# Down projection of a ConvFFN by Strassen's scheme at one level, its weight blocks split by ScalarE, GpSimd and VectorE

## The reference, cut to what matters

```
u = rmsnorm(x, g_pre_ffn) @ w_up                       # 1024 -> 2 * 2816
uc = conv_b + sum over i of u_ext[:, i:i+T] * conv_w[i]   # width 3, per channel
gate, val = uc[..., :2816], uc[..., 2816:]
f = (gelu(gate) * val) @ w_down                        # 2816 -> 1024
x = x + rmsnorm(f, g_post_ffn)
```

## Time and profile before

| | us |
|---|---|
| median of 3 runs (lowest 1851.1, highest 1852.47) | 1851.71 |
| the profiled execution's own time | 1849.15 |
| its span, first to last instruction | 1847.4 |
| PE busy | 1824.8 |
| POOL busy | 1075.4 |
| DVE busy | 923.5 |
| ACT busy | 559.5 |

### The profile page before, as it was taken

The page is one execution under the profiler, slowest core; times in us unless marked ns, Lnnn a source line. Parts: engine busy times, 40 slices in busy tenths (PEclk is TensorE's granted clock), DMA queues, the critical chain, the costliest instruction groups (busy, mean ns, idle before and its releaser), DMA issues.

```text
span 1847.4 us, 33704 instructions
## 1 busy us (share of the span) xinstructions
PE 1824.8 (99%) x14214; PEld 1768.4 (96%) x14214; DVE 923.5 (50%) x1634; ACT 559.5 (30%) x1197; POOL 1075.4 (58%) x996
## 2 busy tenths in 40 slices
PE   9999999999999999999999999999999999999999
PEld 8999889999999999999999998899999999999999
DVE  6666775232755532523556767752336555235143
ACT  4444443112422211202344445430133222112021
POOL 8686534656555555557665864446456555555564
PEclk9999999999999999999999999999999999999999
DMA  5242112233222222223343421222422222222222
GB/s 189 88 132 86 54 42 84 88 120 112 72 90 92 84 89 92 86 80 97 99 143 93 127 87 47 70 66 84 152 81 75 86 92 89 84 92 91 79 86 95
DMA packets 76231, 170.49 MB, mean 92 GB/s; under 512 B 6384, under 2 KB 34160, under 8 KB 76080
## 3 DMA queue, kind: packets, MB, share of 16 engines
q1 hardware_dynamic: 68752, 160.79, 27.1%
q10 hardware_dynamic: 7328, 7.54, 1.2%
HBM read 156.41 MB, written 9.79 MB: 90 GB/s over the span
## 4 chain that ended last, share of the span: by engine, by line
PE 92%; DVE 5%; ACT 1%; POOL 1%; issue 1%; DMA 0%; SPq 0%; DVEq 0%; ACTq 0%; POOLq 0%
PE ps L1579 76%; PE ps L1614 3%; PE ps L1742 2%; PE ps L1700 2%; DVE xn L1101 1%; DVE xT L1446 1%; DVE mix L1443 1%; PE ps L1796 1%; PE ps L1653 1%; PE ps L1802 1%; DVE R L1101 1%; PE ps L1719 1%; DVE xT L1264 1%; PE ps L1668 1%; PE ps L1738 1%
## 5 line engine op out<-in xcount | busy, mean ns | idle before, releaser
L1579 PE MATMUL ps<-xn,wsp 128*128 128x272 f32 x7824 | 1002.0, 289 | 5.7 <-issue 2.2
L1579 PEld LDWEIGHTS ps<-xn,wsp 128*128 128x128 f32 x7824 | 986.1, 189 | 10.8 <-issue 6.0
L616 POOL CAST wsp<-raw 128x1024 fp32r<-128x1024 f32 (+2 forms) x222 | 220.1, 997 | 505.0 <-DMA raw<-in_wstream 450.3
L623 POOL TENSOR_TENSOR wsp<-raw,wsp 128x1024 fp32r<-128x1024 f32 (+2 forms) x278 | 492.1, 1782 | 16.2
L1579 PE MATMUL ps<-R,wsp 128*128 128x272 f32 x3840 | 486.2, 288 | 0.1
L1579 PEld LDWEIGHTS ps<-R,wsp 128*128 128x128 f32 x3840 | 482.7, 188 | 1.2 <-DVE xT L1130 0.5
L610 POOL TENSOR_TENSOR wsp<-raw,wsp 128x256 fp32r<-128x256 f32 x304 | 235.5, 795 | 12.2
L605 POOL CAST wsp<-raw 128x512 fp32r<-128x512 f32 x152 | 112.2, 738 | 147.9 <-DMA raw<-in_wstream 113.3
L1101 DVE SCALAR_TENSOR_TENSOR R<-ps,R 64x256 fp32r<-64x256 f32 (+12 forms) x264 | 130.0, 510 | 73.2 <-ACT R L753 24.6
L1462 DVE TENSOR_TENSOR mix<-ps,rstd 128x272 f32<-128x272 f32 x88 | 38.8, 441 | 202.9 <-PE ps L1579 192.6
L986 ACT ACTIVATE mix<-vv 128x2 f32<-128x2 f32 x88 | 17.9, 204 | 363.0 <-DVE mix L1464 363.0
(11 more groups left out here) (230 smaller groups left out, 1529.2 us busy)
## 6 DMA issues: line engine op xcount, KB each, us to landing
raw<-in_wstream SPq DMA_DIRECT2D x233, 512.0 KB, 3.5
raw<-in_wstream SPq DMA_DIRECT2D x48, 128.0 KB, 2.6
raw<-in_wstream SPq DMA_DIRECT2D x16, 384.0 KB, 3.0
raw<-in_kc SPq DMA_DIRECT2D x8, 512.0 KB, 3.8
raw<-in_vc SPq DMA_DIRECT2D x8, 512.0 KB, 4.8
xT<-in_x_in SPq DMA_DIRECT2D x8, 272.0 KB, 5.3
out_k_out<-mix ACTq DMA_DIRECT2D x8, 272.0 KB, 2.9
xT<-in_x_in SPq DMA_DIRECT2D x1, 2176.0 KB, 9.2
```

Of the source, the lines that this page charges most:

```text
L616: ins = nc.gpsimd.tensor_copy(dst[:, 0, f], part[:, f])
L623: ins = nc.gpsimd.tensor_tensor(dst[:, 1, f], part[:, f], dst[:, 0, f].bitcast(F32), ALU.subtract)
L1579: mm = pe.matmul(z[:, h], w[:, x, (k0 + k) * P:(k0 + k + 1) * P], rhs[:, y, k, h * HT:(h + 1) * HT], start=(k == 0 and (x, y) == (0, 0)), ...
```

## The change

The down product of one part is a product of two matrices, each cut in 2 x 2 blocks: the weights of a pair of output tiles (j, j + 4) and the two halves of the part's features (A11, A12, A21, A22), and the activations by feature half and position half (B11, B12, B21, B22). Strassen's scheme (in Winograd's form) takes 7 block products P1 to P7 in place of 8. For each pair it needs four sums of weight blocks (S1 = A21 + A22, S2 = S1 - A11, S3 = A11 - A21, S4 = A12 - S2), and for each pair of feature tiles four sums of activations (T1 to T4).

- PE: `down_product` runs each product as (number of tiles in half a part: 4, 4 or 3) x 3 parts matmuls of 272 columns into one bank, in the order P1, P5, P6, P2, P7, P3, P4. P6 and P7 go on in P1's bank. Before each goes on, ACT copies the bank's present sum into the bank of P2, P3 or P4 (`hand_on`), and PE waits for that copy.
- DVE: makes the weight sums (`weight_sum`) and the activation sums (`product`), the low parts of five or two activation blocks per tile instead of one, and adds P5, P2, P7, P3, P4 to `fT` (`collect`).
- ACT: makes the high parts of the plain weight blocks A11, A12, A22 (`plain_high`), of the four sums (`sum_high`), of the activation blocks (`g_high`), and the three `hand_on` copies of a pair.
- POOL: for a pair of down chunks it no longer makes high parts; it makes seven low parts of 512 (or 384) columns, in the order `DOWN_LOWS`. All other chunks stay as they were.
- The order of the stages is now up, down, up, down, up, down, with one buffer `g_s` for the split activations. The chunks of a pair stand side by side in the stream. The weight sums S1, S2 and S4 have one buffer each (`s_s`, `ukT`), S3 lies in the slot of chunk j + 4. DVE, ACT and POOL do the sums of the first pair of a part between the up tiles of its last feature tile `end`.

```diff
-FFN = _up(0) + _up(1) + _down(0) + _up(2) + _down(1) + _down(2)
+FFN = _up(0) + _down(0) + _up(1) + _down(1) + _up(2) + _down(2)
...
+DOWN_LOWS = ("A11", "S1", "S3", "A22", "S2", "A12", "S4")
...
+                        if ch[0] == "down":
...
+                            for n in DOWN_LOWS:
+                                pool.wait_ge(pre["sum_hi"], highs_made(layer, i, j, n))
+                                pool.wait_ge(pre["sum_raw"], sums_made(layer, i, j, {"A11": "S3", "S1": "S2", "S3": "S3", "A22": "S1"}.get(n, "S4")))
+                                nc.gpsimd.tensor_tensor(lo[n], whole_sum[n], hi[n].bitcast(F32), ALU.subtract).then_inc(S["w_lo"], 1)
...
+                    def sum_high(i, j, n):
+
+                        if (i, j) != (0, 0):
+                            act.wait_ge(S["p_done"], AT[({"S1": "P5", "S2": "P6", "S3": "P7", "S4": "P3"}[n], *pair_before(i, j))] + 1)
+                        act.wait_ge(pre["sum_raw"], sums_made(layer, i, j, n))
+                        ac(down_parts(layer, i, j, 0)[n], down_sums(layer, i, j)[n], ACT.Copy).then_inc(pre["sum_hi"], 1)
...
+                    def hand_on(i, j, n, to):
+
+                        act.wait_ge(S["dve_read"], max(dread(o) for o in BEFORE[(to, i, j)]))
+                        act.wait_ge(S["p_done"], AT[(n, i, j)] + 1)
+                        ac(bank((to, i, j))[:, 0:HT], bank(("P7", i, j))[:, 0:HT], ACT.Copy).then_inc(S["act_read"], 1)
...
+                            if j == end:
+                                plain_high(i, 0)
+                                for n in ("S1", "S2", "S3"):
+                                    sum_high(i, 0, n)
+                            u_tile(("upg", j))
+                            if j == end:
+                                sum_high(i, 0, "S4")
+                            u_tile(("upv", j))
+                            if j == end:
+                                hand_on(i, 0, "P1", "P2")
+                            act.wait_ge(S["conv2"], 2 * j + 1)
+                            ac(gel, uc[0], ACT.Gelu_apprx_tanh).then_inc(S["gelu_done"], 1)
+                            g_high(j, (lambda: hand_on(i, 0, "P6", "P3")) if j == end else None)
...
+                    def weight_sum(i, j, n):
...
+                        v.scalar_tensor_tensor(a[n], a[x], 1.0, a[y], ALU.mult, ALU.add if n == "S1" else ALU.subtract).then_inc(pre["sum_raw"], 1)
...
+                            if j == end:
+                                for n in ("S1", "S2", "S3"):
+                                    weight_sum(i, 0, n)
+                            if j != 1:
+                                u_tile(("upg", j))
+                            if j == end:
+                                weight_sum(i, 0, "S4")
+                            if j > _F0[i]:
+                                lows_left(j - 1, (G_B22, G_T3))
+                            taps(("upg", j))
+                            u_tile(("upv", j))
...
+                            else:
+                                pe.wait_ge(S["act_read"], aread(({"P6": "P1", "P2": "P1", "P7": "P6", "P3": "P6", "P4": "P7"}[n], i, j)))
+                        for k in ks:
+                            if j == 0:
+                                pe.wait_ge(S["g_lo"], G_LO[_F0[i] + k + (0 if opens else h), DOWN_ON[n]])
+                            for x, y in PARTS:
+                                mm = pe.matmul(z, w[x][:, k * P:(k + 1) * P], g_s[:, y, k, DOWN_ON[n]],
+                                               start=(opens and k == 0 and (x, y) == (0, 0)), stop=(k == h - 1 and x == 1),
+                                               skip_group_check=True)
```

More of the change, by code:

```diff
@@ L50, in _down @@
 def _down(i):
-    return [("down", i, j) for j in range(KT)]
-FFN = _up(0) + _up(1) + _down(0) + _up(2) + _down(1) + _down(2)
+    return [("down", i, j + n) for j in range(NP) for n in (0, NP)]
+FFN = _up(0) + _down(0) + _up(1) + _down(1) + _up(2) + _down(2)
 CHUNKS += FFN + [(n, j) for j in range(KT) for n in ("pleg", "plep")]
@@ L82, in ring_slot, with lows @@
     return (layer * NST + ST_AT[c]) % SLOTS
+DOWN_LOWS = ("A11", "S1", "S3", "A22", "S2", "A12", "S4")
+def lows(c):
+    return sum((len(DOWN_LOWS) if m[2] >= NP else 0) if m[0] == "down" else 1 for m in STREAM[:ST_AT[c] + 1])
 def chunk_floats(c):
@@ L361, in build @@
             EVENTS.append(("done", t))
-        whole(("nm", 2), *FFN[2:], ("plep", 4), ("nm", 3), ("plep", 5), ("plep", 6), ("plep", 7))
+        whole(("nm", 2))
+        for i in range(len(FFN_PARTS)):
+            whole(*_up(i)[2 if i == 0 else 0:])
+            EVENTS.append(("turn", None))
+            for j in range(NP):
+                EVENTS += [("lend", ("P7", i, j)), ("done", ("P1", i, j)), ("lend", ("P5", i, j)), ("done", ("P5", i, j)),
+                           ("lend", ("P2", i, j)), ("done", ("P6", i, j)), ("lend", ("P3", i, j)), ("done", ("P2", i, j)),
+                           ("lend", ("P4", i, j)), ("done", ("P7", i, j)), ("done", ("P3", i, j)), ("done", ("P4", i, j))]
+        whole(("plep", 4), ("nm", 3), ("plep", 5), ("plep", 6), ("plep", 7))
         for j in range(3):
@@ L432, in last_tile @@
                 return ("plep", KT // 2 * (c[1] + 1) - 1)
+            if c[0] == "down":
+                return ("P2", c[1], c[2]) if c[2] < NP else ("P4", c[1], c[2] - NP)
             return c
@@ new lines, in sum_high, with plain_high @@
+                    def sum_high(i, j, n):
[3 more added lines that the diff above has]
+                        ac(down_parts(layer, i, j, 0)[n], down_sums(layer, i, j)[n], ACT.Copy).then_inc(pre["sum_hi"], 1)
+                    def plain_high(i, j):
+                        w = FFN_PARTS[i] * P
+                        for n, m, f in (("A11", j, slice(0, w)), ("A22", j + NP, slice(w // 2, w))):
+                            slot = ring_slot(layer, ("down", i, m))
+                            act.wait_ge(raw_in[slot], 16 * LOADS[layer * NST + ST_AT[("down", i, m)]])
+                            ac(wsp[:, slot, 0, f], raw[:, slot, 1, f], ACT.Copy).then_inc(pre["sum_hi"], 1)
@@ new lines, in collect @@
+                    def collect(i, n, j, places, new):
+                        t = (n, i, j)
+                        dve.wait_ge(S["p_done"], AT[t] + 1)
+                        if n == "P7":
+                            dve.wait_ge(S["act_read"], aread(t))
+                        for m, h in places:
+                            f, z = fT[:, m, h * HT:(h + 1) * HT], bank(t)[:, 0:HT]
+                            if i == 0 and new:
+                                ins = v.tensor_copy(f, z)
+                            else:
+                                ins = v.tensor_tensor(f, z, f, ALU.add)
+                        ins.then_inc(S["dve_read"], 1)
```

316 lines of the change are left out of this document (224 added, 92 removed).

## The result

The changed kernel takes **1882.51 us** (median of 4 runs, 1881.08 to 1882.9) against 1851.4 (1849.68 to 1852.47) for the kernel before on the same chip: 1.0167 times as long, 95% interval 1.015 to 1.0185. The profiled execution took 1881.08 us with a span of 1879.3, 31.9 more than before. With the matmuls removed worth 33.1 us, 65.0 us are newly lost on PE. Only 43.0 of them are idle time of PE (span less busy time: 65.6 now, 22.6 before); the other 22.0 lie in matmuls that took longer than their spacing. PE's busy time fell by 11.1 us and not by 33.1.

The account below looks back on a forecast made before the run. PE was taken as the bound, busy 99%. From 1849.15, 33.1 us of matmuls removed and 70.8 of new waits (76.8 at full lock, partly halved) gave 1886.9, so 1889 us for the median; range 1846 to 1908.

Parts of the forecast that it names:

- The list of waits: New PE waits in six down stages: 4 x 12.8 + 2 x 11.8 us with the lock, 4 x 5.3 + 2 x 6.2 without.
- three signs of being wrong: P6's first wait in a part under 2 us, last value tile read within 1.5 us, or clock row under 1.00.
- Removal, -33.1 us: Down projections: 132 fewer matmuls per layer, 264 in all, at 125.4 ns each.
- The lock: DVE instructions with two SBUF inputs and POOL's hold each other up; DVE's take 1 to 2 us instead of 0.45 to 0.65.
- P6 on the copy of P1, 5.2 us a part: First pair of 8-tile parts: P6 waits for ACT's copy behind the late value tile, 5.2 us with P5's small wait.
- T2's 1.3 us: First pair of 8-tile parts: PE waits 1.3 us for T2's low part after the 18 matmuls of P6 and P2.
- P4 on the copy of P7, 1.9 us: First pair of 8-tile parts: the copy stands behind next-pair work on ACT and DVE, so P4 waits 1.9 us.
- Pair to pair, 4.1 us: P6 of pairs 1 to 3 waits for POOL's low part of S2: 4.1 us, 1.0 without the lock.
- Part 2's first pair, 8.0 us: Waits at the start of the 6-tile part's down stage: 8.0 us, 5.3 without the lock.
- where I had 2 on POOL: Behind part 2, POOL comes about 1 us late with chunk ("plep", 4), once per layer; none without the lock.
- The clock, a rival at 0.13: TensorE falls to 1.2 GHz behind the long wait; 24 matmuls cost 3.0 us more per part, 18 us, 1907; chance 0.13.
- The rival that it pays, 1828: DVE reads the last value tile by t = 1.5, only the last T2 is late, 9 us of waits: 1828; chance 0.14.

Follow-up runs that it names:

- Experiment 3: Changed kernel with two memsets on POOL in place of each low-part subtraction of the down weights, PE multiplying by the high part: 1858.61 us.
- experiment 2: Changed kernel with POOL making only 32 columns of each low part of the down weights, PE multiplying by the high part instead: 1850.57 us.
- experiment 9: experiment 8 plus ACT's value tile before its P6 copy, S4's high part earlier, POOL held for T2 in part 2, last projection chunk in halves: 1855.66 us.
- experiment 10: experiment 9 plus POOL's first-pair low parts reordered, S4's held until T3's in part 2, ACT making three later chunks' high parts: 1850.73 us.
- experiment 7: Changed kernel with S4 in its own buffer and POOL's low parts reordered, plus DVE and ACT reordered around the end tile: 1873.93 us.
- experiment 8: experiment 7 plus the next up stage's first two tiles placed between last product and down stage in parts 0 and 1: 1873.24 us.

## Why the prediction was right, and where it wasn't

The direction and the mechanism hold, and the number is close: 1889 forecast, 1882.5 measured, 65.0 us newly lost against 70.8. But the closeness of the number is in good part luck. The list of waits was about twice too long (4 x 12.8 + 2 x 11.8 = 74.8 us for the six down stages, 38.4 measured), and 21.5 us in them and 5.1 outside that it did not have made up for most of that. Two of the prediction's three signs of being wrong came: P6's first wait in a part is under 2 us in part 2 (1.65 and 1.64), and the clock's row falls under 1.00.

- **Removal, -33.1 us: right.** 264 fewer, and the rest keep their spacing: between the down stages 96.22 us for 768 (617.17 to 713.39), 125.3 ns each.
- **The lock: right, and what turns no change into a slowdown.** Experiment 3 isolates it for DVE's sums before P6. Without POOL's low parts 34.4 us are lost (experiment 2), where the same list gave 33.6; with them 65.0, where I had 70.8. The 33.6 too fits better than the list deserves: only 19.2 of the 34.4 are waits in the down stages.
- **P6 on the copy of P1, 5.2 us a part: too high.** Measured 2.20, 3.04, 2.62 and 2.28 in the four parts with 8 tiles. S4, B22 and T3 beside POOL cost 4.16 us (711.61 to 715.77), and the prediction's list has about the same. What was off is mostly the start: the activation sums before them end at -4.5 and not -3.25, since POOL is idle for 14.44 us before the down stage and could hold up none of them; I had POOL busy there as in the up stages before. The value tile is read at 4.7 instead of 6.7: 1.2 of these 2 us are the start, the rest small sizes behind it. T2's 1.3 us measured 1.12, 0.18 and twice none. The 1.12 is the stage at clock 1.00; in the other three P6 and P2 run at 0.50 before it, and that time covers T2's wait.
- **P4 on the copy of P7, 1.9 us: right,** 1.61 in each of these parts. It is 1.61 without POOL's low parts too (experiments 2 and 3), so the lock has no share in it.
- **Pair to pair, 4.1 us: too high.** 1.03 and 0.24. POOL's seven low parts take 9.64 us (728.77 to 738.41), not 11.4, since DVE's sums seldom hold them up, and only the second pair is late by a full microsecond. In part 2 it is 3.2 us against 3.8.
- **Part 2's first pair, 8.0 us: too high,** 1.65 + 1.88 + 0.20 + 0.51 = 4.2.
- **The term that was missing.** The listed waits in the six down stages sum to 38.4 us. But the stages last 291.4 us for 1848 matmuls, worth 231.6: 59.9 lost. 1.2 of the 21.5 between are DVE's sums before ("plep", 4), where I had 2 on POOL. The rest is what a wait costs beyond its own length. In the first stage, at clock 1.00, six waits of 6.39 us in all go with 50.61 - 42.1 = 8.5 us, so about 0.35 us more for each. The rows show where: the 12 matmuls before a wait take 1.67 us (714.89) and the 12 behind one 1.71 (735.52 to 737.23), in place of 1.50. I had charged each wait its idle time alone.
- **The clock, a rival at 0.13: it happened, at a fraction of its price.** It is at 0.50 behind the first waits in five of the six stages, all but the first. Two stages of 8 tiles with and without can be compared: 9.8 - 6.3 = 3.5 us beyond the waits with the fall (part 1) and 2.1 without (part 0), so about 1.4 us each and some 7 in all by estimate, where I had 3.0 each for 24 matmuls at half speed. It was at 0.50 for 3.4 us (720.8 to 724.2), too short for 24. And some 3 of the 7 are no loss, because they stand where T2's waits would have been: the three parts with 8 tiles in which the clock fell waited 0.18 us, 0 and 0 for T2, against 1.12.
- **Outside the stages, 5.1 us not foreseen.** 3.5 of them are the residual stage's waits on xn, 10.2 us where there were 6.7, with its POOL work now later and beside DVE's sums (experiments 9 and 10). The granted clock falls there too, in layer 0: 0.58 in the mean from 891 to 894, behind a wait of 1.98 us.
- **The rival that it pays, 1828:** its condition, the value tile read by t = 1.5, was met in experiment 7 (1.1) and didn't pay, because the lock now met sum T2 behind it, which the rival had left out.

Open: how the 24 us between experiment 3 and the change divide into the lock and the longer parts; how much of experiment 3's 8 us is POOL's length and how much its later end at the residual stage; and whether fewer POOL columns, or the low parts on another engine, would bring the removal's 33 us home. It wasn't tried.

## What to carry to other kernels

Before trading matmuls for sums on VectorE, look at what GpSimd is queued to read at that moment, and price the sums at GpSimd's durations, not their own. Take away a wait only after asking where the other engine's queue then lies: in experiments 7 and 8 it met the next instructions. Charge PE for each new stop somewhat more than its idle time (here about 0.35 us). Holding back the other engine by a wait of its own is worth trying, but in experiment 9 it only moved PE's wait to the next low part.

## What the runs showed of the hardware

- Turns are taken instruction by instruction: a VectorE sum of 272 columns with both inputs in SBUF takes 0.44 us alone and 1.50 to 1.53 beside queued GpSimd subtractions of 512 columns (1.26 to 1.30 us alone), which themselves grow to 1.46 and 1.74.
- A GpSimd memset (0.53 us for 512 columns) beside such sums lengthens none of them: 0.68 and 0.43 us (experiment 3).
- The granted clock fell to 0.50 after waits of 3.04, 2.62 and 2.28 us and, in part 2, after 1.65 and 1.88 us close together, but not after 2.20 and 1.12 us in the first stage. The length of the waits alone doesn't decide it: in experiment 8 waits of 1.08 and 2.00 us stand in the same places of parts 0 and 1, and in both layers the clock fell behind them in part 0 and stayed at 1.00 in part 1. Windows behind the 2.62 us wait, then of experiment 8 in part 0 and part 1:

```profile
1507.00:1509.00 2.00, 2.00 (x11) 2.00 (x11) 1.91 (x5) 1.18 (x3) 0.00 (x0) 0.50 0.00 0
...
595.00:599.00 4.00, 4.00 (x22) 4.00 (x21) 0.30 (x1) 1.86 (x3) 4.00 (x5) 0.57 0.02 5
740.00:745.00 5.00, 5.00 (x42) 5.00 (x41) 1.97 (x3) 1.87 (x3) 5.00 (x5) 1.00 0.09 37
```

The Trainium skill, "TensorE: Matmul & The Clock Gate", section "Why this matters for your kernels", says that longer idle gaps between bursts bring the clock back to half. The trace agrees in five stages; in the sixth, with gaps nearly as long, it stayed at 1.00.
